# A transformer kernel's entry to differential attention: product order on PE, half-row adds and squares

## What is computed

```python
h = h + mla_mixer(...)
return rms_norm(h, g_final)
```

```python
h = layer_norm(x, ln_in_g, ln_in_b)
for l in range(DEPTH):
    proj = jnp.einsum('bsd,de->bse', h, w_in[l])      # q, k, v, u: 512 columns each
    a = diff_attention(q, k, v, lam, lam_init, subln_g[l])
    f = fourier_mix(u, w_f[l], b_f[l])
    mix = jnp.einsum('bse,ed->bsd', jnp.concatenate([a, f], axis=-1), w_o[l])
    h = layer_norm(ALPHA * h + mix, ln1_g[l], ln1_b[l])
    h = layer_norm(ALPHA * h + swiglu(h, w_gu[l], w_down[l]), ln2_g[l], ln2_b[l])
```

## Time and profile before

| | |
|---|---|
| median of 3 runs | 923.92 us (923.88 to 924.03) |
| the profiled execution | 923.47 us |
| its span, first to last instruction | 921.7 us |
| PE, PEld, DVE, ACT, POOL busy | 98%, 83%, 64%, 53%, 12% of the span |
| mean granted TensorE clock | 0.998 |
| HBM read | 149.72 MB, 164 GB/s over the span |

### The profile page before, as it was taken

How to read it: one execution, slowest core, us unless ns; L and a number is a source line. 1 busy time by engine, 2 the same in 40 slices (tenths; PEclk the granted TensorE clock), 3 DMA queues, 4 the chain that set the end, 5 groups by cost and what they waited for, 6 DMA issues and landing times.

```text
span 921.7 us, 13498 instructions
## 1 busy us (share of the span) xinstructions
PE 905.3 (98%) x4954; PEld 764.8 (83%) x4954; DVE 594.4 (64%) x1082; ACT 486.5 (53%) x791; POOL 115.1 (12%) x108
## 2 busy tenths in 40 slices
PE   9999999999999999999999999999999999999996
PEld 7999878889888869887888888887978788888885
DVE  4898677687668585867654544557585855545444
ACT  4955757466786463763543434335574454334431
POOL 4643863102000000002000000000001100000000
PEclk9999999999999999999999999999999999999999
DMA  9655232663533127232565455444332355555521
GB/s 352 231 203 177 87 122 76 228 229 138 212 109 138 58 96 315 96 128 97 193 237 191 174 214 192 175 145 183 139 137 92 135 215 198 183 182 183 192 83 46
DMA packets 22379, 151.59 MB, mean 164 GB/s; under 512 B 2608, under 2 KB 3120, under 8 KB 4528
## 3 DMA queue, kind: packets, MB, share of 16 engines
q1 hardware_dynamic: 20304, 142.62, 42.7%
q10 hardware_dynamic: 2016, 8.16, 2.3%
HBM read 149.72 MB, written 1.05 MB: 164 GB/s over the span
## 4 chain that ended last, share of the span: by engine, by line
PE 57%; DVE 3%; ACT 2%; issue 1%; POOL 0%; DVEq 0%; POOLq 0%; ACTq 0%
PE ps L514 12%; PE ps L516 12%; PE ps L520 12%; PE ps L1137 5%; PE ps L817 2%; PE ps L819 2%; PE ps L818 2%; PE ps L1155 2%; PE ps L563 1%; PE ps L1199 1%; PE ps L547 1%; PE ps L545 1%; PE ps L543 1%; PE ps L859 1%; DVE wlo L1808 1%
## 5 line engine op out<-in xcount | busy, mean ns | idle before, releaser
L1323 ACT CAST whi<-raw 128x2048 fp32r<-128x2048 f32 (+1 forms) x127 | 241.3, 1905 | 146.1 <-PE ps L520 109.8
L1808 DVE TENSOR_TENSOR wlo<-raw,whi 128x1024 fp32r<-128x1024 f32 x127 | 162.3, 1278 | 140.0 <-ACT whi L1323 139.5
L514 PE MATMUL ps<-whi,ahi 128*128 128x512 f32 (+2 forms) x448 | 173.5, 387 | 0.0
L516 PE MATMUL ps<-wlo,ahi 128*128 128x512 f32 (+2 forms) x448 | 172.0, 384 | 0.0
L520 PE MATMUL ps<-whi,alo 128*128 128x512 f32 (+2 forms) x448 | 170.9, 384 | 0.0
L1814 DVE TENSOR_TENSOR wlo<-raw,whi 128x1024 fp32r<-128x1024 f32 x107 | 130.5, 1220 | 0.0
L514 PEld LDWEIGHTS ps<-whi,ahi 128*128 128x128 f32 x448 | 84.2, 188 | 16.9 <-issue 0.8
L516 PEld LDWEIGHTS ps<-wlo,ahi 128*128 128x128 f32 x448 | 84.2, 188 | 16.4 <-issue 0.5
L520 PEld LDWEIGHTS ps<-whi,alo 128*128 128x128 f32 x448 | 84.2, 188 | 16.3
L514 PE MATMUL ps<-whi,bhi 128*128 128x512 f32 x174 | 69.7, 401 | 0.4 <-issue 0.3
L543 PE MATMUL ps<-ahi,whi 128*128 128x256 f32 x240 | 68.4, 285 | 0.0
(11 more groups left out here) (291 smaller groups left out, 1727.0 us busy)
## 6 DMA issues: line engine op xcount, KB each, us to landing
raw<-in_wstream SPq DMA_DIRECT2D x133, 1024.0 KB, 4.8
par<-in_params ACTq DMA_DIRECT2D x5, 1024.0 KB, 5.2
tab<-in_tables ACTq DMA_DIRECT2D x1, 1370.0 KB, 11.7
res<-in_x SPq DMA_DIRECT2D x2, 512.0 KB, 4.3
raw<-in_wstream SPq DMA_DIRECT2D x2, 512.0 KB, 6.9
out<-res SPq DMA_DIRECT2D x4, 256.0 KB, 2.1
par<-in_params ACTq DMA_DIRECT2D x1, 512.0 KB, 3.7
arena<-in_wf ACTq DMA_DIRECT2D x2, 256.0 KB, 4.8
```

The lines of the kernel that those rows point to most:

```text
L514: pe.matmul(banks[b][:, 0:cw], h_, wh[:, i, c], start=st, stop=False, skip_group_check=True)
L516: pe.matmul(banks[b][:, 0:cw], h_, wl[:, i, c], start=False, stop=False, skip_group_check=True)
L1323: act.copy(whi[:, u % SPL, c], raw[:, u % RAW, c]).then_inc(w_hi, 1)
L1808: dve.tensor_tensor(wlo[:, u % SPL, c], raw[:, u % RAW, c], whi[:, u % SPL, c].bitcast(F32), ALU.subtract).then_inc(w_lo_v, 1)
```

## The change

In PE's order, layer 0: `o_half(3, 1, 1)` stands before the turn of tile 0 in the place of the fill, and the folded products stand after that turn, ahead of `v_products(0, 0)`. Layer 1: the folded products take the place of the fill after `v_products(0, 0)`, and four high-by-high products of the second value unit for tile 0 stand before the turn of tile 1. In both layers the products of the second value unit are taken apart by `v_rest(t, a, w)`, four matmuls each: low activations by high weights and high by high stand earlier, those with the low rests of the weights last. All products are made once, as before.

On ACT the sums of squares are made by half row (`first_square`, into `fsum`, signal `fsq`), and the two of tile 1 stand around the casts of tile 0; `ln_square(0, 1)` stands ahead of the cast of `("vu", 0, 1)`. The cast of `("qk", l, 0)` stands behind the casts of tile 1. On DVE `gained_half(1, 0)` stands before `stretch(0, 0)`, and `gained_half(1, 1)` and `mean(1)` before `tile_lo(("h", 0), 0)`; the centring waits for `fsq`. POOL adds the two half sums before it scales them.

```diff
--- before.py
+++ after.py
@@ -308,6 +308,7 @@
         oss = scal(2 * NH)
         ors = scal(2 * NH)
         lsum = scal(2 * T)
+        fsum = scal(2 * T)
         nmean = scal(T)
         nmean_s = scal(T)
         lvar = scal(T)
@@ -393,6 +394,7 @@
         y_head, dx_done, y_raw, z_copied, z_silu = (
             sem("y_head"), sem("dx_done"), sem("y_raw"), sem("z_copied"), sem("z_silu"))
         y_gated, y_norm = sem("y_gated"), sem("y_norm")
+        fsq = sem("fsq")
         acc_psum, acc_read, lead_t0 = sem("acc_psum"), sem("acc_read"), sem("lead_t0")
         gate_done = sem("gate_done")
         gate_tanh, half_done = sem("gate_tanh"), sem("half_done")
@@ -1071,9 +1073,8 @@
             o_half(3, 1, 0).then_inc(acc_psum, 1)
             o_half(1, 1, 1)
             o_half(2, 1, 1)
-            keep_busy(X[0], 2)
+            o_half(3, 1, 1)
             turn_tile_when(("h", 0), 0)
-            o_half(3, 1, 1)
 
             def lead_units(names, fills, banks, acc):
 
@@ -1096,16 +1097,44 @@
                     return tile_products(("vu", l, i), t, ahi, alo, range(4 * i, 4 * i + 4), 4, 512, [G[2 + t]],
                                          i == 0, i == 1)
 
+                def v_rest(t, a, w):
+
+                    wait_emptied(pe, FILL["h", l, t, 1])
+                    u = UNIT["vu", l, 1]
+                    pe.wait_ge(w_hi, u + 1)
+                    if w is wlo:
+                        unit_ready(("vu", l, 1))
+                    for k in range(4):
+                        mm = pe.matmul(G[2 + t], a[:, 4 + k, t * P:(t + 1) * P],
+                                       w[:, u % SPL, k * 512:(k + 1) * 512], start=False,
+                                       stop=w is wlo and k == 3, skip_group_check=True)
+                    return mm
+
+                def fold():
+
+                    pe.wait_ge(wf_in, 16 * (l + 1))
+                    for q, name in enumerate(("cos_c", "nsin_c")):
+                        pe.matmul(X[q], const(name), wfs, start=True, stop=True).then_inc(f_fold, 1)
+
+                if l == 0:
+                    fold()
                 pe.wait_ge(acc_read, 4 * (1 + 2 * l) + 2)
                 v_products(0, 0)
-                keep_busy(X[0], 2)
+                if l:
+                    fold()
+                    v_rest(0, ahi, whi)
                 turn_tile_when(("h", l), 1)
-                pe.wait_ge(wf_in, 16 * (l + 1))
-                for q, name in enumerate(("cos_c", "nsin_c")):
-                    pe.matmul(X[q], const(name), wfs, start=True, stop=True).then_inc(f_fold, 1)
+                if l:
+                    v_rest(0, alo, whi)
+                else:
+                    v_rest(0, ahi, whi)
                 v_products(0, 1).then_inc(w_used, 1)
-                v_products(1, 0).then_inc(lead_t0, 1)
-                v_products(1, 1).then_inc(w_used, 1)
+                if l == 0:
+                    v_rest(0, alo, whi)
+                v_rest(1, ahi, whi)
+                v_rest(1, alo, whi)
+                v_rest(0, ahi, wlo).then_inc(lead_t0, 1)
+                v_rest(1, ahi, wlo).then_inc(w_used, 1)
                 turned(("qk", l, 0), ahi, alo, G[0])
                 turned(("qk", l, 2), ahi, alo, G[1])
 
@@ -1359,7 +1388,7 @@
 
                 act.wait_ge(ln_mean, T * n + t + 1)
                 if n == 0:
-                    act.wait_ge(sq_done, T * N_F + t + 1)
+                    act.wait_ge(fsq, 2 * t + 2)
                 if T * n + t:
                     act.wait_ge(ln_var, T * n + t)
                 act.activation(junk[:, t, :], xsum[:, t, :], ACT.Square, scale=D ** -0.5,
@@ -1645,15 +1674,24 @@
             act.wait_ge(q_rope, 3 * T)
             load_wf(0)
 
-            def first_norm(t):
-                ln_square(0, t)
-                if t == 0:
-                    tile_hi(("h", 0), 0)
-                    split.until(("vu", 0, 1), 0)
+            def first_square(t, b):
+
+                act.wait_ge(acc_read, 4 + 2 * t + b + 1)
+                if (t, b) == (0, 0):
+                    act.wait_ge(sq_done, T * N_F)
+                c = slice(b * 512, (b + 1) * 512)
+                act.activation(junk[:, t, c], res[:, t, c], ACT.Square,
+                               accum_out=fsum[:, 2 * t + b:2 * t + b + 1]).then_inc(fsq, 1)
 
             split.until(("vu", 0, 0), 0)
-            squares(N_F, lambda t: res[:, t, :], D, lambda t: act.wait_ge(acc_read, 4 + 2 * (t + 1)),
-                    first_norm)
+            first_square(0, 0)
+            first_square(0, 1)
+            ln_square(0, 0)
+            first_square(1, 0)
+            tile_hi(("h", 0), 0)
+            first_square(1, 1)
+            ln_square(0, 1)
+            split.until(("vu", 0, 1), 0)
             dscale = HD ** -0.5
             for l in range(DEPTH):
                 if l:
@@ -1661,10 +1699,10 @@
                     ln_square(2 * l, 0)
                     tile_hi(("h", l), 0)
                     split.until(("vu", l, 1), 0)
-                split.until(("qk", l, 0), 0)
                 if l:
                     ln_square(2 * l, 1)
                 tile_hi(("h", l), 1)
+                split.until(("qk", l, 0), 0)
                 for q in range(2):
                     act.wait_ge(f_fold, 2 * l + q + 1)
                     act.copy(cw[:, q, :], X[q]).then_inc(cw_done, 1)
@@ -2325,24 +2363,24 @@
                     ins.then_inc(r_final, 1)
                     dve.wait_ge(r_final, t + 1)
 
-            def first_variance(t):
-
-                mean(t)
-                dve.wait_ge(rs_done, T * N_F + t + 1)
+            def first_centre(t):
+
+                dve.wait_ge(fsq, 2 * t + 2)
+                centre(0, t)
 
             params_ready(0)
             params_ready(1)
             split.until(("vu", 0, 0), 0)
             gained_half(0, 0)
             gained_half(0, 1)
-            first_variance(0)
-            centre(0, 0)
+            mean(0)
+            first_centre(0)
+            gained_half(1, 0)
             stretch(0, 0)
-            gained_half(1, 0)
+            gained_half(1, 1)
+            mean(1)
             tile_lo(("h", 0), 0)
-            gained_half(1, 1)
-            first_variance(1)
-            centre(0, 1)
+            first_centre(1)
             stretch(0, 1)
             tile_lo(("h", 0), 1)
             split.until(("vu", 0, 1), 0)
@@ -2585,10 +2623,10 @@
             root(N_CKV, KV_LORA)
             root(N_CQ, Q_LORA)
             for t in range(T):
-                pool.wait_ge(sq_done, T * N_F + t + 1)
+                pool.wait_ge(fsq, 2 * t + 2)
                 a = ssq[:, 2 * N_F + t:2 * N_F + t + 1]
-                pool.tensor_scalar(a, a, LN_EPS / D, LN_EPS * EPS, ALU.mult, ALU.add).then_inc(rs_done, 1)
-                pool.wait_ge(rs_done, T * N_F + t + 1)
+                link(pool.tensor_tensor(a, fsum[:, 2 * t:2 * t + 1], fsum[:, 2 * t + 1:2 * t + 2], ALU.add))
+                link(pool.tensor_scalar(a, a, LN_EPS / D, LN_EPS * EPS, ALU.mult, ALU.add))
                 root_ln(0, (t,), a)
             for l in range(DEPTH):
                 for t in range(T):
```

## The result

The changed kernel took **918.63 us** (median of 4 runs, 918.28 to 918.89) beside 923.90 us for the kernel before (923.83 to 924.03): a ratio of 0.9941, 95% interval 0.9929 to 0.9954. It is faster by 5.3 us. The forecast was 918.0 us in a range of 917.0 to 920.6. The profiled execution of the changed kernel took 918.89 us, 0.26 over its median; its span is 917.1 us.

The account below looks back on a forecast made before the run. PE's instruction stream was taken as the bound, busy 98% of the span. Gains of 3.9 us (layer 0) and 2.2 (layer 1) less 0.2 gave 5.9 us, hence a 918.0 us median, range 917.0 to 920.6.

Parts of the forecast that it names:

- Layer 0, tile 0: First tile's norm and transposes: no gain, `stretch` at 329.42 against 329.47, transposes at 330.23, fold done by 332.88.
- the new wait: Layer 0, after the fold: first value products wait for `tile_lo` and start at 333.37, 0.49 us after the fold.
- Layer 0, tile 1: Second tile's norm: `ln_square` near 332.95 instead of 335.3, transposes at 336.27; q/k at 345.75, a gain of 3.9 us.
- `stretch` starts at 332.95 + 2.51: Layer 0's second tile: `stretch` follows `ln_square` by the earlier chain's 2.51 us, so at 335.46.
- The POOL pair at zero: Layer 0: POOL's add and scale of the half sums cost nothing; without cover, 1.1 us for the pair.
- Layer 1: Second entry: fold replaces fill, all eight transposes run at once; q/k at 638.13 against 640.32, a gain of 2.2 us.
- What takes something back: Before layer 0's first scores: loads and ACT's casts lose 0.2 us, bounds 0 and 1.9; parameter loads about 1 us earlier.
- Rival (a): q/k unit 3's load lands as late as before, PE waits 1.9 us at first scores: 919.7 us, chance 0.17.
- the sum for the scores: Layer 0, before first scores: ACT's two casts and two copies end near 358.5 if the load lands by 353.3.
- the prediction's own limit of 337.5: Layer 0: the forecast counts as wrong if tile 1's transposes start after 337.5 us.
- Rival (d): Without fill the clock falls to 1.2 GHz in both entries, 8.2 us lost each: 934.4 us, chance 0.02.
- My evidence against it: Layer 0 before: no slower matmul followed 2.5 us of idling and transposes; new stretches without matmuls are shorter.

Follow-up runs that it names:

- pair_dve: Changed kernel with POOL's new add of the half sums and its scaling moved to VectorE, POOL keeping the root; 919.09 us, ratio 0.9949.
- qk_cast: Changed kernel with the q/k unit's cast again ahead of tile 1's variance (layer 1) and tile 1's casts (layer 0); 918.70 us, ratio 0.9944.
- l0_norm: Kernel before with only layer 0's half squares and new ScalarE, VectorE and POOL orders, PE's order and fills as before; 926.44 us, ratio 1.0021.
- l0_pe: Kernel before with only PE's new order in layer 0, whole squares and the other engines' orders as before; 923.58 us, ratio 0.9993.
- no_fill: Kernel before without its fill products, nothing put in their place; 924.14 us, ratio 1.0014.
- hh_early: Changed kernel with layer 0's four high-by-high products of the second value unit moved ahead of tile 1's transposes; 917.91 us, ratio 0.9936.
- hi_first: Changed kernel with layer 0's high-by-high products before tile 1's transposes, first value products high activations first, tile 1 centred before tile 0's low parts; 917.67 us.

## Why the prediction was right, and where it was off

The time lay inside the range, 0.6 us over the forecast, and the forecast's mechanism is the one that the traces show. Step by step, with the 0.63 us that the profiled execution brought along taken off:

**Layer 0, tile 0**: right to 0.01 us up to the transposes. `ln_square` 326.64 (326.63 forecast), `stretch` 329.43 (329.42), transposes 330.23 (330.23): no gain, since the moved add eats the earlier variance. The fold came next, and the first value product at 333.37 is the forecast's number, 0.80 us behind the start of `tile_lo` (0.79 forecast): the new wait was there, some 0.4 us by the fold's start and length.

**Layer 0, tile 1**: the step that failed is "`stretch` starts at 332.95 + 2.51". `ln_square` was in time, 332.87. But from it to `stretch` took 336.61 - 333.50 = 3.11 us. I had taken 2.51 us from tile 0 as a constant of the chain. But it held POOL's scale at 0.33 us, which met only the last 0.2 us of VectorE's centring; in the new order the centring stands behind `tile_lo`, starts 0.91 us after `ln_square` instead of 0.30, and lies beside the whole scale, which took 0.93 us. The difference, 0.60 us, is all that the chain was longer by. The transposes came at 336.79 instead of 336.27, and q/k at 346.22 instead of 345.75: **3.45 us instead of 3.9**. The POOL pair at zero was right: it was done at 333.97, 0.94 us before the scale, and pair_dve shows that taking it off POOL helps nothing. The rest was right: from the transposes' start to q/k 9.43 us, forecast 9.48.

What held the scale is a pair of instructions that don't run side by side: POOL's small operation and VectorE's centring, whose two large inputs (`arena` and `par`) are both in SBUF. `tile_lo`, which reads PSUM and `ahi`, ran beside the pair's scale at 333.78 and left it at 0.19 us. The Trainium skill (SBUF — State Buffer, "Who interferes with whom") says that a VectorE instruction with two inputs in SBUF contends with a GpSimd instruction that reads SBUF, because its second input comes through a read interface that the two share. The traces agree: 0.30 us alone, 0.92 to 1.35 us beside the centring when the scale begins in its first half. That this interface is the cause rather than something else the two share was not tested by itself.

**Layer 1**: 1.92 us instead of 2.2. Fold and four products up to the transposes took 2.64 us (forecast 2.49), transposes and 32 products 8.51 us (forecast 8.39): two terms slightly too small. That the transposes would run without a wait was right. That the q/k cast had to go to get there was not needed, as qk_cast shows.

**What takes something back**: forecast 0.2 us, measured nothing. The parameter loads left ACT at 338.94 and 339.32, 2.7 us earlier than before and not 1, and the load of q/k landed 2.37 us earlier. Rival (a) falls: both sides of the traffic moved with the entry. And ACT had time to spare: its last copy ahead of the scores waited 1.38 us for PE, 1.94 us in the kernel before, which the sum for the scores had left out.

Together: 5.9 - 0.47 (tile 1) - 0.27 (layer 1) + 0.2 (scores) - 0.16 (lost between 360 and 625 us, not followed up) - 0.63 (in this execution, before the entry) = 4.57 us, and the two profiled executions differ by 4.58. Without the 0.63 us the same sum gives 5.20 us, and the medians give 5.3 and 5.4. In the profiled execution tile 1's transposes stood at 337.42, just under the prediction's own limit of 337.5 for a forecast that is wrong; without the late arrival it is 336.79.

**Rival (d)**, the clock, did not come about in the changed kernel, but its mechanism is real: l0_norm, l0_pe and no_fill leave PE idle for 2.5 to 2.7 us in one piece. In l0_norm's trace the clock falls to 0.50 after it, and the times and mean clocks of some executions of the other two fit the same fall. My evidence against it, that no slower matmul followed the gap of the earlier trace rows, was weaker than I took it for: that gap held a fill and 0.99 us of idling. What speaks against it is the longest idle time in the new entries, 0.42 us. Its price was set too high: the one fall in l0_norm was over within about 5 us, and whole executions with a low mean clock took 1.5 to 3.4 us more than the fastest of their kernel (l0_pe, no_fill), not 8.2 us for each entry. The Trainium skill (TensorE: Matmul & The Clock Gate, "What's actually happening") has the clock throttled by default and released by activity; the rows of l0_norm, 0.50 at 338 to 340 us behind the idling and 1.00 from 342 us on, agree with that.

## What to carry to other kernels

In these runs fill in front of a wait was free, and without it executions with a lower mean clock came up. Removing it paid only together with something that made the wait itself shorter, and then in full. By the medians neither half of this change gave anything in layer 0 alone (923.6 and 926.4 us beside 924.05), both gave 3.7 us. Put real work that is ready early in the gap, on both sides of the instruction that is waited for, as hh_early did for another half microsecond. When a chain of small operations is copied from one tile to the next in a sum, look at what the neighbour engine does beside each link; here one link of 0.33 us became 0.93.

## What the runs showed that was not expected

A 128x1 scale on POOL took 0.19 to 0.30 us alone or beside `tile_lo`, and 0.92 to 1.35 us when it began early in a 1024-wide centring of VectorE with both large inputs in SBUF; it ended 0.16 or 0.17 us after that instruction (0.06 us in hi_first). The centring is not the only such partner. The longest scale stands in the profile of the kernel before: 2.02 us beside two subtractions of VectorE (`wlo<-raw,whi`, L1808 and L1814, 163.78 to 166.15), 0.05 us behind the second:

```profile
164.18 2.02 POOL L2521 TENSOR_SCALAR small<-small 128x1 f32<-128x1 f32 x1 [7.44 <-ACT arena L1352]
```

It depends on a few tenths of a microsecond who meets whom: at 151 us the scale took 0.76 us in one profile of the changed kernel and 0.19 us in the other, which shifted all that came after by some 0.4 us. That this is the same collision fits (VectorE was in a group of additions with both inputs in SBUF, and the long scale ended 0.05 us behind the last of them) but was only argued; in the profile of before the scale took 0.19 us beside the same additions.

An idle stretch of 2.5 to 2.7 us on PE doesn't always bring the clock down. By times and mean clocks it did in six of eleven executions of l0_pe and in five of eleven of no_fill; the profiled executions of both show none. A single profile of such a kernel shows one of two times (922.2 us at a mean clock of 0.999 for l0_pe, where the median was 923.58 us; 927.07 us for l0_norm, where the fastest was 925.16), so it takes the list of times and clocks to see what the idling costs.
